# First slots of a two-layer encoder trunk: splits from transposed tiles in PSUM, transposes between products, and squares summed a slot sooner

## The chip, the core and the metric

The kernel runs on one core of one Trainium2 chip. The metric is the device time of one execution in microseconds (us). TensorE (PE) has its weight loads shown apart (PEld); VectorE is DVE, ScalarE ACT, GpSimd POOL, SyncE SP.

## What is computed

Two consecutive layers of a hybrid encoder on 256 tokens, with 16 learned meta tokens ahead of them (T = 272), width 2048, float32. Layer 0 runs 2-D neighbourhood attention and bidirectional mLSTM heads beside each other, layer 1 gated linear attention; each is followed by a gated ConvFFN. Every sub-layer is pre-RMSNorm with a residual add. What matters here are two starts, each a norm followed by a projection:

```python
def _rms(x, gain):
    xf = x.astype(jnp.float32)
    y = xf * lax.rsqrt(jnp.mean(xf * xf, axis=-1, keepdims=True) + EPS)
    return (y * gain.astype(jnp.float32)).astype(x.dtype)

# layer 0:  _split(rms(x) @ w_in, EVEN_SIZES)      the opening: mLSTM columns first
# both layers, _conv_ffn(h, ...):
u = h @ w_up                                       # then a 3-tap convolution over tokens
g, val = jnp.split(acc, 2, axis=-1)
return (jax.nn.silu(g) * val) @ w_down
```

## The kernel before

Activations are kept transposed, features on partitions: `h` is 16 tiles of 128 x 272, the residual. Every float32 operand of a projection is split into a high and a low half: `act_hi` = h x gain rounded (`norm_high`, ACT, L594), `act_lo` = h x gain - act_hi (`norm_low`, DVE, L1046); weights likewise, `w_hi` on ACT (`hi`, L539, writing `hi_done`) and `w_lo` on DVE (`lo`, L942, writing `split_done`). A product is three matmuls, high x high, low x high and high x low (L1455 to L1457). The factor 1/rms per token is left out of the halves; it is applied as each output leaves PSUM (`evac`, L949, by `rstd`), so the sum of squares is needed only then.

A projection runs in iterations of eight slots (`gemm`, `body`). A slot is a weight block of four k tiles by two output tiles, 512 KB in one of four buffers of `raw`: 24 matmuls. For `full` projections slots 0 to 3 make output group 0 (PSUM banks 0 and 1) and slots 4 to 7 group 1 (banks 2 and 3). SP's `fetch` (L405) of a slot waits until the slot four before is split. In slot s of its program ACT makes the high weight half of slot s + 3, DVE the low one. Each engine runs its own queue in order; what runs beside a projection are generators, advanced one step a slot (`side`, `beside`).

In the first iteration behind a norm (`late=True`) the groups leave only in slots 6 and 7, because `rstd` comes late: `norm_side` squares four tiles a slot on ACT (L613), adds them up on DVE one slot after (`sum_squares`, L1063; three long sums, then two short ones), lets PE multiply the sum by ones behind slot 5 (L1498), takes the root on ACT in slot 6 and the reciprocal on DVE in slot 6, ahead of that slot's weight half. `ffn_stage` (L812, L1392, L1765) runs `up00`, `down00` and so on; `NORM_EARLY` says how many tiles of the halves are made in the last iteration of the projection before (8 for norms 1 and 3). A conv exit is long: DVE moves two tiles out of PSUM (L976), ACT applies the middle tap (L558), DVE the two others (L984, L989), and for group 1 ACT's SiLU and DVE's gate and split follow.

The opening: SP loads x in five parts (`X_PARTS`), a weight slot behind each but the first. PE multiplies ones by ones 20 times (`WARM`, L1751), transposes the gains, then turns x tile by tile into PSUM banks 4 to 7 (`turn_in`, L1476; three transposes a tile): tiles 0 to 7 ahead of the products, 8 to 11 behind slot 0 and 12 to 15 behind slot 1. In four rounds DVE copies two tiles into `h` (`fill_h`, L1367) and ACT two (L796); the halves are then made from `h`, and one weight slot is split per round, slots 3 and 4 behind them (L791, L1371). The first iteration's `norm_side(0)` follows, with 11 small DMA issues on ACT's queue (`load_more`, L528), and behind its ones product a matmul group for the gate columns (the tail, L1504).

Of the kernel before, what the change touches and what calls it, by code (L numbers as in the profile page):

```python
# [95 lines left out]
def build(nc, x, meta_tokens, norm_mix, norm_ffn, ab_w_in, ab_gate_bias, ab_q_gain, ab_k_gain,  # L96
# [54 lines left out]
    with ctx:  # L151
# [101 lines left out]
        all_sems = """const_done gain_in warm_ready param_in conv_in tail_in c_tail_in meta_in gup_in hi_done split_done used bank_free u_ready conv_mid gates_done  # L253
# [110 lines left out]
        WARM = 20  # L364
        X_PARTS = [(0, 2), (2, 2), (4, 4), (8, 4), (12, 4)]
# [38 lines left out]
        def _(sp):  # L404
# [17 lines left out]

            for q, (k0, kn) in enumerate(X_PARTS):
                c0, n = k0 * P, kn * P
                sp.dma_start(tok[:, 1:3, c0:c0 + n],
                             bass.AP(x.tensor, x.offset + c0, [[D, P], [P * D, 2], [1, n]])).then_inc(S(f"tok_in{q}"), 16)
                if q:
                    fetch(gemms[0], 0, q - 1, wait=False)
# [75 lines left out]
        def _(act):  # L504
# [60 lines left out]
            def gemm(g, first=None, beside=None, last_beside=None):  # L565
                def body(i, nxt, ni, side=None, late=False):
                    for s in range(8):
# [7 lines left out]
                        if late:  # L575
                            if s >= 6:
                                evac(g, i, s - 6)
                        elif s % g["gs"] == g["gs"] - 1:
                            evac(g, i, s // g["gs"])

                last, start = g["iters"] - 1, 0
                if first:
                    body(0, g, 1, first, late=True)
                    finish(first)
                    start = 1
# [14 lines left out]

            def norm_early(n):
# [11 lines left out]
            def norm_side(n):  # L613

                for q in range(4):
# [3 lines left out]
                    A(sq[:, 4 * q:4 * q + 4, :], h[:, 4 * q:4 * q + 4, :], ACT.Square).then_inc(S("sq_ready"), 1)  # L619
# [5 lines left out]
                yield  # L625
                if n == 2:
# [176 lines left out]
            for s in range(3, 3 + gemms[0]["ahead"]):  # L803
                hi(gemms[0], 0, s)
# [7 lines left out]
            def ffn_stage(layer, n):  # L812
                norm(n)
                gemm(G[f"up{layer}0"], first=norm_side(n))
# [117 lines left out]
        def _(dve):  # L932
# [3 lines left out]
            V.memset(ones[:, :], 1.0).then_inc(S("warm_ready"), 1)  # L936
            dve.sem_inc(S("const_done"), 1)
# [73 lines left out]
            def gemm(g, first=None, beside=None, last_beside=None):  # L1011
                per = 7 if g["evac"] == "conv" else g["ng"] if g.get("wide") else 0

                def body(i, nxt, ni, side=None, late=False):
                    for s in range(8):
# [7 lines left out]
                        if late:  # L1023
                            if s >= 6:
                                evac(g, i, s - 6)
# [4 lines left out]
                if first:  # L1030
                    body(0, g, 1, first, late=True)
# [335 lines left out]
            def fill_h(k):  # L1367
                dve.wait_ge(S("xT_done"), k + 2)
                V.tensor_copy(h[:, k:k + 2, :], ps[:, 4:6, 0:T]).then_inc(S("h_dve"), 1)

            for q in range(4):  # L1371
                fill_h(4 * q)
                if q == 0:
                    dve.wait_ge(S("par_evac"), 1)
# [453 lines left out]
```

## Time and profile before

| | us |
|---|---|
| median of 3 runs | 2412.82 |
| all runs | 2408.90, 2412.82, 2415.22 |
| the profiled execution, device time | 2412.13 |
| its span, first to last instruction | 2410.3 |
| PE busy (products and weight loads overlap) | 2374.9 |
| DVE busy | 1623.4 |
| ACT busy | 1181.4 |
| mean granted TensorE clock, 1 being 2.4 GHz | 0.992 |

Busy shares and the chain are sums over the whole span. To see a start, one reads the timeline of that stretch and engine: each row has the start, the duration, the instruction, and in brackets how long the engine was idle before it and what released it. The table of stretches gives PE's granted clock between two times.

### The profile page before, as it was taken

What the parts mean: (1) busy time and instruction counts of PE and PEld (TensorE: products, weight loads), DVE (VectorE), ACT (ScalarE), POOL (GpSimd) and SP (SyncE); (2) the same over time, 40 slices, a digit from 0 to 9 for tenths busy, and PEclk for the clock granted to TensorE, in tenths of its full rate; (3) what the DMA queues carried; (4) which work ended last, traced back from release to release, by engine and by line L of the source; (5) the groups of instructions that cost most, each with busy time, mean ns of one, the idle gap of its engine ahead of it and who ended that gap; (6) DMA issues with size and microseconds to landing.
All of it is one profiled execution on the core that took longest, in us unless ns stands there. A gap on an engine that the chain in (4) does not pass through costs nothing.

```text
span 2410.3 us, 50498 instructions
## 1 busy us (share of the span) xinstructions
PE 2374.9 (99%) x19342; PEld 2291.6 (95%) x19342; DVE 1623.4 (67%) x2333; ACT 1181.4 (49%) x1563; POOL 34.8 (1%) x78
## 2 busy tenths in 40 slices
PE   9999989999999999999999999999999999999999
PEld 7998887999999999999999999999999999999998
DVE  5447796677765776577574666766777667766774
ACT  5344645554543444454458633454545445544543
POOL 0000001000000000000002000000000000000000
PEclk9999999999999999999999999999999999999999
DMA  6654455555565565655665544456565656666665
GB/s 183 191 145 126 132 144 125 169 167 184 190 201 184 176 207 182 195 182 183 193 182 152 158 123 114 122 155 205 167 200 192 206 185 193 203 200 190 209 194 164
DMA packets 430780, 420.26 MB, mean 174 GB/s; under 512 B 26082, under 2 KB 428812, under 8 KB 430636
## 3 DMA queue, kind: packets, MB, share of 16 engines
q1 hardware_dynamic: 416720, 415.29, 55.9%
q10 hardware_dynamic: 13932, 3.17, 1.2%
q8 instruction: 92, 1.51, 0.3%
q14 instruction: 36, 0.29, 0.0%
HBM read 416.31 MB, written 2.10 MB: 174 GB/s over the span
## 4 chain that ended last, share of the span: by engine, by line
PE 89%; DVE 6%; ACT 3%; issue 2%; ACTq 0%; DVEq 0%
PE ps L1457 27%; PE ps L1455 24%; PE ps L1456 24%; PE ps L1453 6%; DVE w_lo L946 2%; PE ps L1687 1%; ACT w_hi L545 1%; PE ps L1681 1%; PE ps L1526 1%; PE ps L1525 1%; PE ps L1504 1%; DVE rt L1145 1%; DVE rt L1153 1%; PE ps L1527 0%; ACT act_hi L599 0%
## 5 line engine op out<-in xcount | busy, mean ns | idle before, releaser
L1455 PE MATMUL ps<-act_hi,w_hi 128*128 128x272 f32 (+1 forms) x4864 | 1371.3, 282 | 10.2 <-DVE w_lo L946 8.8
L1456 PE MATMUL ps<-act_lo,w_hi 128*128 128x272 f32 (+1 forms) x4864 | 1354.5, 278 | 0.0
L1457 PE MATMUL ps<-act_hi,w_lo 128*128 128x272 f32 (+1 forms) x4864 | 1354.4, 278 | 0.0
L946 DVE TENSOR_TENSOR w_lo<-raw,w_hi 128x1024 fp32r<-128x1024 f32 (+1 forms) x800 | 946.3, 1203 | 477.9 <-ACT w_hi L545 450.0
L545 ACT ACTIVATE w_hi<-raw 128x1024 fp32r<-128x1024 f32 (+1 forms) x797 | 815.4, 1035 | 684.8 <-PE ps L1457 652.1
L1455 PEld LDWEIGHTS ps<-act_hi,w_hi 128*128 128x128 f32 x4864 | 929.0, 191 | 18.6 <-issue 10.0
L1456 PEld LDWEIGHTS ps<-act_lo,w_hi 128*128 128x128 f32 x4864 | 929.0, 191 | 1.5
L1457 PEld LDWEIGHTS ps<-act_hi,w_lo 128*128 128x128 f32 x4864 | 928.8, 191 | 0.0
L1457 PE MATMUL ps<-g_both,w_lo 128*128 128x272 f32 (+1 forms) x1408 | 388.3, 276 | 0.0
L1457 PEld LDWEIGHTS ps<-g_both,w_lo 128*128 128x128 f32 x1408 | 268.2, 190 | 0.0
L1453 PE MATMUL ps<-g_both,w_hi 128*128 128x512 f32 x704 | 231.5, 383 | 0.0
L558 ACT ACTIVATE acc<-un,conv 128x272 f32<-128x272 f32 (+1 forms) x176 | 97.2, 599 | 236.9 <-DVE un L976 236.9
L1455 PE MATMUL ps<-g_both,w_hi 128*128 128x272 f32 x704 | 196.4, 279 | 0.0
L1456 PE MATMUL ps<-g_both,w_hi 128*128 128x272 f32 x704 | 196.4, 279 | 0.0
L984 DVE SCALAR_TENSOR_TENSOR acc<-un,conv,acc 128x271 f32<-128x271 f32 (+1 forms) x176 | 78.9, 490 | 124.5 <-ACT acc L558 124.5
L1453 PEld LDWEIGHTS ps<-g_both,w_hi 128*128 128x128 f32 x704 | 133.1, 189 | 18.2
L1455 PEld LDWEIGHTS ps<-g_both,w_hi 128*128 128x128 f32 x704 | 133.1, 189 | 0.0
L1456 PEld LDWEIGHTS ps<-g_both,w_hi 128*128 128x128 f32 x704 | 133.1, 189 | 0.0
L976 DVE TENSOR_TENSOR un<-ps,rstd 128x544 f32<-128x544 f32 (+1 forms) x88 | 62.4, 709 | 28.2 <-PE ps L1457 27.6
L989 DVE SCALAR_TENSOR_TENSOR acc<-un,conv,acc 128x271 f32<-128x271 f32 (+1 forms) x176 | 78.3, 486 | 0.0
L960 DVE TENSOR_TENSOR h<-ps,h 128x544 f32<-128x544 f32 (+4 forms) x80 | 56.6, 707 | 16.1 <-PE ps L1457 15.2
L1298 DVE TENSOR_TENSOR proj_all<-proj_all,bc 128x272 f32<-128x272 f32 (+1 forms) x112 | 40.8, 421 | 0.0
(250 smaller groups left out, 1182.8 us busy)
## 6 DMA issues: line engine op xcount, KB each, us to landing
raw<-in_ffn_w_up SPq DMA_DIRECT2D x352, 512.0 KB, 4.6
raw<-in_ffn_w_down SPq DMA_DIRECT2D x128, 512.0 KB, 4.2
raw<-in_ab_w_in SPq DMA_DIRECT2D x96, 512.0 KB, 3.8
raw<-in_c_w_in SPq DMA_DIRECT2D x96, 512.0 KB, 3.8
raw<-in_ffn_w_down SPq DMA_DIRECT2D x64, 384.0 KB, 4.0
raw<-in_ab_w_out SPq DMA_DIRECT2D x32, 512.0 KB, 3.4
raw<-in_c_w_out SPq DMA_DIRECT2D x32, 512.0 KB, 4.3
bias<-in_ab_rel_bias ACTq DMA_DIRECT2D x32, 64.0 KB, 5.1
```

The source lines that it names most:

```text
L545: A(w_hi[:, s % 4, 0:kc * 256], raw[:, s % 4, 0:kc * 256], ACT.Copy).then_inc(S("hi_done"), 1)
L558: ins = A(acc[:, grp, m, o0:T], un[:, grp, m, o0:T], ACT.Identity, bias=conv[:, g["layer"], 3, bass.ds(mt, 1)], scale=conv[:, g["layer"], ...
L946: V.tensor_tensor(w_lo[:, s % 4, 0:kc * 256], raw[:, s % 4, 0:kc * 256], w_hi[:, s % 4, 0:kc * 256].bitcast(F32), ALU.subtract).then_inc(S ...
L960: V.tensor_tensor(hh, banks, hh, ALU.add).then_inc(S("bank_free"), 1)
L976: V.tensor_tensor(un[:, grp, :, t0:T], banks, rs, ALU.mult).then_inc(S("u_ready"), 1)
L984: before.append(chain.mark(V.scalar_tensor_tensor(acc[:, grp, m, b1:T], un[:, grp, m, b1 - 1:T - 1], wt[0][:, bass.ds(mt[m], 1)], acc[:, g ...
L989: ins = V.scalar_tensor_tensor(acc[:, grp, m, o0:T - 1], un[:, grp, m, o0 + 1:T], wt[2][:, bass.ds(mt[m], 1)], acc[:, grp, m, o0:T - 1], A ...
L1298: ins = V.tensor_tensor(o, o, total_of(a[d], l, not right), ALU.mult)
L1453: mm(o2, wh, g_both[:, kk, :, :, t0 // 2:].rearrange("p c a b -> p c b a"), start=(c == 0 and k == 0), stop=False)
L1455: mm(o, wh, moving(xh, kk), start=(c == 0 and k == 0), stop=False)
L1456: mm(o, wh, moving(xl, kk), start=False, stop=False)
L1457: ins = mm(o, wl, moving(xh, kk), start=False, stop=end)
```

## The change

In the opening: the 20 products of ones go. x is loaded in eight pairs of tiles, weight slots 0 to 3 behind pairs 0, 2, 4 and 6. PE turns pairs 0 to 2 ahead of the products; pairs 3 to 7 each follow half a slot of products, whose order is changed to two k tiles by two outputs, and half a slot waits for two `act_lo` tiles, not four. Pairs take PSUM banks 4-5, 6-7 and 2-3 in turn. `act_hi` and `act_lo` are made from PSUM; the copies into `h` come behind them (even pairs DVE, odd pairs ACT) and hold the bank. Weight slot 0 is split ahead of the first halves, and each next one a pair or so ahead of its use.

For norms 1 and 3 (`SOON`: `up00` and `up10`): the squares of tiles 0 to 7 and their sum move into slots 4 to 6 of the last iteration of the projection before; squares 2 and 3, the remaining sums, PE's ones product, root and reciprocal come one slot sooner; and group 0 leaves in slot 5 instead of 6 (`SOON_LATE`). Norms 0 and 2 keep their slots.

```diff
-        WARM = 20
-        X_PARTS = [(0, 2), (2, 2), (4, 4), (8, 4), (12, 4)]
+        SOON = (1, 3)
+        LATE, SOON_LATE = {6: 0, 7: 1}, {5: 0, 7: 1}
+        PAIR_BANK = [4 if p % 3 == 0 else 6 if p % 3 == 1 else 2 for p in range(KT // 2)]
+        FETCH_AFTER = {0: 0, 2: 1, 4: 2, 6: 3}
...
@@ SP
-            for q, (k0, kn) in enumerate(X_PARTS):
-                c0, n = k0 * P, kn * P
+            for p in range(KT // 2):
+                c0, n = 2 * p * P, 2 * P
...
-                if q:
-                    fetch(gemms[0], 0, q - 1, wait=False)
+                if p in FETCH_AFTER:
+                    fetch(gemms[0], 0, FETCH_AFTER[p], wait=False)
...
@@ body on ACT and DVE
                         if late:
-                            if s >= 6:
-                                evac(g, i, s - 6)
+                            if s in late:
+                                evac(g, i, late[s])
...
@@ ACT
             def norm_early(n):
...
+                if n in SOON:
+                    for q in range(2):
+                        square(q)
+                        yield
...
             def norm_side(n):
-                for q in range(4):
+                for q in range(2 if n in SOON else 0, 4):
...
                 yield
+                if n in SOON:
+                    yield
...
-            for q in range(4):
-                act.wait_ge(S("h_dve"), q + 1)
-                norm_high(0, 4 * q)
-                norm_high(0, 4 * q + 1)
-                act.wait_ge(S("xT_done"), 4 * q + 4)
-                A(h[:, 4 * q + 2:4 * q + 4, :], ps[:, 6:8, 0:T], ACT.Copy).then_inc(S("h_act"), 1)
-                if q < 3:
-                    act.wait_ge(landed[q], 16)
-                    A(w_hi[:, q, :], raw[:, q, :], ACT.Copy).then_inc(S("hi_done"), 1)
-                act.wait_ge(S("h_act"), q + 1)
-                norm_high(0, 4 * q + 2)
-                norm_high(0, 4 * q + 3)
-            for s in range(3, 3 + gemms[0]["ahead"]):
-                hi(gemms[0], 0, s)
+            def first_high(p):
+
+                act.wait_ge(S("xT_done"), 2 * p + 2)
+                for k in (2 * p, 2 * p + 1):
+                    A(act_hi[:, k, :, :], parted(ps[:, PAIR_BANK[p] + k % 2, 0:T]), ACT.Copy,
+                      scale=vec[:, V_MIX + k:V_MIX + k + 1]).then_inc(S("x_hi"), 1)
...
+            def fill_odd(p):
+
+                act.wait_ge(S("act_ready"), 2 * p + 2)
+                b = PAIR_BANK[p]
+                A(h[:, 2 * p:2 * p + 2, :], ps[:, b:b + 2, 0:T], ACT.Copy).then_inc(S("h_act"), 1)
+
+            first_weights(0)
+            for p in range(KT // 2):
+                first_high(p)
+                if p in (1, 3, 5):
+                    first_weights((p + 1) // 2)
+                if p % 2 == 0 and p:
+                    fill_odd(p - 1)
+            hi(gemms[0], 0, 4)
+            fill_odd(7)
...
@@ DVE
             def norm_early(n):
...
+                if n in SOON:
+                    yield
+                    yield
+                    sum_squares(n, 1)
+                    yield
...
             def norm_side(n):
-                for t in range(6):
-                    if 2 <= t < 5:
-                        sum_squares(n, t - 1)
-                    if t == 4:
+                soon = n in SOON
+                for t in range(5 if soon else 6):
+                    if 2 - soon <= t < 5 - 2 * soon:
+                        sum_squares(n, t - 1 + 2 * soon)
+                    if t == 4 - soon:
                         sum_squares(n, 4)
                         sum_squares(n, 5)
...
+            lo(gemms[0], 0, 0)
+            for p in range(KT // 2):
+                first_low(p)
+                if p in (1, 3, 5):
+                    lo(gemms[0], 0, (p + 1) // 2)
+                if p % 2 == 0:
+                    b = PAIR_BANK[p]
+                    V.tensor_copy(h[:, 2 * p:2 * p + 2, :], ps[:, b:b + 2, 0:T]).then_inc(S("h_dve"), 1)
+            lo(gemms[0], 0, 4)
...
@@ PE
+                        opening = isinstance(n, int) and n == 0 and s < 4
...
+                        pairs = [(m, k) for m in range(2) for k in range(kc)]
+                        if opening:
+                            pairs = [(m, k) for k0_ in (0, 2) for m in range(2) for k in (k0_, k0_ + 1)]
+                        for j, (m, k) in enumerate(pairs):
+                            if opening and j % 4 == 0:
+                                pe.wait_ge(S("act_ready"), k0 + k + 2)
...
+                            if opening and j % 4 == 3 and 2 * s + j // 4 + 3 < KT // 2:
+                                turn_in(2 * s + j // 4 + 3)
...
+            def turn_in(p):
+
+                pe.wait_ge(S(f"tok_in{p}"), 16)
+                if p == 0:
+                    pe.wait_ge(S("meta_in"), 16)
+                if p == 2:
+                    pe.wait_ge(S("par_evac"), 1)
+                if p >= 3:
+                    pe.wait_ge(S("act_ready"), 2 * (p - 3) + 2)
+                    pe.wait_ge(S("h_act" if (p - 3) % 2 else "h_dve"), (p - 3) // 2 + 1)
+                for k in (2 * p, 2 * p + 1):
+                    for tt, (t0, tn) in enumerate(TILES):
+                        ins = tr(ps[:, PAIR_BANK[p] + k % 2, t0:t0 + tn], tok[0:tn, tt, k * P:(k + 1) * P], ident[0:tn, 0:tn])
+                    ins.then_inc(S("xT_done"), 1)
...
             def norm_side(n):
-                for t in range(5):
-                    if n == 0 and t < 2:
-                        for k in range(8 + 4 * t, 12 + 4 * t):
-                            turn_in(k)
+                for t in range(4 if n in SOON else 5):
                     yield
...
-            for n in range(WARM):
-                mm(ps[:, 3, 0:P], ones[:, :], ones[:, :], start=True, stop=True)
...
-            for k in range(8):
-                turn_in(k)
+            for p in range(3):
+                turn_in(p)
```

## Rows read from the trace of the kernel before

**Rows 1.** The page: chain that ended last, shares of the span by engine
```profile
PE 89%; DVE 6%; ACT 3%; issue 2%; ACTq 0%; DVEq 0%
```

**Rows 2.** Waits of TensorE: engine line <- waited for: us in all, times, longest
```profile
PE ps L1455 <- DVE w_lo L946: 8.8, 4, 3.1
```

**Rows 3.** Timeline of PE: start us, us, instruction, idle before and releaser
```profile
30.90 0.35 PE L1455 MATMUL ps<-act_hi,w_hi 128*128 128x272 f32 x1 [2.12 <-DVE w_lo L946]
...
529.14 0.38 PE L1455 MATMUL ps<-act_hi,w_hi 128*128 128x272 f32 x1 [2.68 <-DVE w_lo L946]
...
1344.78 1.35 PE L1681 MATMUL ps<-proj_all 128*16 128x16 f32 x12 [1.67 <-DVE proj_all L971]
...
1725.46 0.58 PE L1455 MATMUL ps<-act_hi,w_hi 128*128 128x258 f32 x1 [3.13 <-DVE w_lo L946]
```

**Rows 4.** Stretches of PE: from:to and us, PE busy (x), granted clock, DMA, GB/s
```profile
7.40:11.20 3.80, 3.50 (x21) 1.00 1.07 388
13.98:18.05 4.07, 4.07 (x18) 0.50 0.79 262
31.70:35.10 3.40, 3.40 (x18) 0.50 0.94 254
...
530.05:533.46 3.41, 3.41 (x17) 0.50 0.82 238
...
1725.46:1731.50 6.04, 6.04 (x28) 0.50 0.72 219
...
1343.00:1352.00 9.00, 7.33 (x66) 1.00 0.44 120
```

**Rows 5.** Timeline of ACT in steady running, after 60 us
```profile
61.12 1.06 ACT L545 ACTIVATE w_hi<-raw 128x1024 fp32r<-128x1024 f32 x1 [1.72 <-PE ps L1457]
```

**Rows 6.** Timeline of DVE in up00, and one row of ACT in up10
```profile
501.07 1.23 DVE L946 TENSOR_TENSOR w_lo<-raw,w_hi 128x1024 fp32r<-128x1024 f32 x1 [1.45 <-ACT w_hi L545]
...
513.92 1.84 DVE L1091 RECIPROCAL rstd<-rstd 128x272 f32<-128x272 f32 x1
...
521.75 0.72 DVE L976 TENSOR_TENSOR un<-ps,rstd 128x544 f32<-128x544 f32 x1
...
1705.16 1.06 ACT L545 ACTIVATE w_hi<-raw 128x1024 fp32r<-128x1024 f32 x1 [1.13 <-DMA raw<-in_ffn_w_up]
```

**Rows 7.** Timeline of PE and ACT in the opening
```profile
1.13 6.26 PE L1752 MATMUL ps<-ones 128*128 128x128 f32 x40 [1.13 <-DVE ones L936]
...
10.26 0.60 ACT L796 ACTIVATE h<-ps 128x544 f32<-128x544 f32 x1
...
11.00 1.63 PE L1485 MATMUL ps<-ident,tok 16*128 16x16 f32 x6 [0.16 <-ACT h L796]
...
13.98 0.57 PE L1455 MATMUL ps<-act_hi,w_hi 128*128 128x272 f32 x1 [1.36 <-DVE act_lo L1050]
...
18.91 2.19 PE L1485 MATMUL ps<-ident,tok 16*128 16x16 f32 x12
```

**Rows 8.** DMA issues in the opening: KB, us from issue (1.30, 1.84) to landing
```profile
tok<-in_meta_tokens ACTq DMA_DIRECT2D x1, 128.0 KB, 5.6
...
raw<-in_ab_w_in SPq DMA_DIRECT2D x1, 512.0 KB, 6.6
```

**Rows 9.** Groups by line and form: xcount | busy us, mean ns
```profile
L599 ACT ACTIVATE act_hi<-h,vec 128x272 fp32r<-128x272 f32 x64 | 31.0, 541 | 12.5 <-DVE h L1369 8.3 <-PE ps L1457 4.2
...
L1050 DVE SCALAR_TENSOR_TENSOR act_lo<-h,vec,act_hi 128x272 fp32r<-128x272 f32 x64 | 28.9, 498 | 3.5 <-ACT act_hi L599 3.5
...
L1129 DVE SCALAR_TENSOR_TENSOR ml_p<-ps,ml_x 128x272 f32<-128x272 f32 x16 | 6.3, 434 | 0.0
```

**Rows 10.** Timeline of DVE and PE at the opening's sums
```profile
32.47 1.29 DVE L1068 TENSOR_TENSOR sq<-sq 128x1088 f32<-128x1088 f32 x1 [0.59 <-ACT sq L619]
...
39.41 1.20 DVE L1071 TENSOR_TENSOR sq<-sq 128x544 f32<-128x544 f32 x2
...
40.98 0.62 PE L1498 MATMUL ps<-sq,ones 128*128 128x272 f32 x2
```

More of the change, by code:

```diff
@@ L582, in gemm @@
                 if first:
-                    body(0, g, 1, first, late=True)
+                    body(0, g, 1, first, late)
                     finish(first)
@@ L599, in norm_high, with square @@
                 A(act_hi[:, k, :, :], parted(h[:, k, :]), ACT.Copy, scale=vec[:, v0 + k:v0 + k + 1]).then_inc(S("x_hi"), 1)
+            def square(q):
+                A(sq[:, 4 * q:4 * q + 4, :], h[:, 4 * q:4 * q + 4, :], ACT.Square).then_inc(S("sq_ready"), 1)
             def norm_early(n):
@@ L618, in norm_side @@
                         act.wait_ge(S("h_act"), q + 1)
-                    A(sq[:, 4 * q:4 * q + 4, :], h[:, 4 * q:4 * q + 4, :], ACT.Square).then_inc(S("sq_ready"), 1)
+                    square(q)
                     if n == 0:
@@ L813, in ffn_stage @@
                 norm(n)
-                gemm(G[f"up{layer}0"], first=norm_side(n))
+                gemm(G[f"up{layer}0"], first=norm_side(n), late=SOON_LATE)
                 gemm(G[f"down{layer}0"])
@@ L1030, in gemm @@
                 if first:
-                    body(0, g, 1, first, late=True)
+                    body(0, g, 1, first, late)
                     finish(first)
@@ L1365, in low_gla, with first_low @@
                                 ALU.subtract).then_inc(S("act_ready"), 1)
[L1367 to L1374, printed above, removed]
[L1375 to L1384 removed]
+            def first_low(p):
+                for k in (2 * p, 2 * p + 1):
+                    dve.wait_ge(S("x_hi"), k + 1)
+                    V.scalar_tensor_tensor(act_lo[:, k, :, :], parted(ps[:, PAIR_BANK[p] + k % 2, 0:T]), vec[:, V_MIX + k:V_MIX + k + 1],
+                                           act_hi[:, k, :, :].bitcast(F32), ALU.mult, ALU.subtract).then_inc(S("act_ready"), 1)
+            lo(gemms[0], 0, 0)
[7 more added lines that the diff above has]
+            lo(gemms[0], 0, 4)
             mixers = even()
@@ L1393, in ffn_stage @@
                 norm(n)
-                gemm(G[f"up{layer}0"], first=norm_side(n))
+                gemm(G[f"up{layer}0"], first=norm_side(n), late=SOON_LATE)
                 gemm(G[f"down{layer}0"])
@@ L1437, in body @@
                             pe.wait_ge(S("bank_free"), i * g["ng"] + (g["gr0"] + grp + 1))
-                        if grp == 0:
+                        opening = isinstance(n, int) and n == 0 and s < 4
+                        if grp == 0 and not opening:
                             if mid:
@@ L1445, in body @@
                             o = ps[:, 2 * (grp % 2) + m, 0:T - t0]
                             o2 = ps[:, 2 * (grp % 2) + m, :].rearrange("p (a b) -> p a b", a=2)
[L1447 to L1457 removed]
+                            kk = g["x0"] + k0 + k
@@ new lines, in body @@
+                            w0 = k * 256 + m * P
+                            wh, wl = w_hi[:, s % 4, w0:w0 + P], w_lo[:, s % 4, w0:w0 + P]
+                            end = c == g["gs"] - 1 and k == kc - 1
+                            if g.get("wide"):
+                                mm(o2, wh, g_both[:, kk, :, :, t0 // 2:].rearrange("p c a b -> p c b a"), start=(c == 0 and k == 0), stop=False)
+                            else:
+                                mm(o, wh, moving(xh, kk), start=(c == 0 and k == 0), stop=False)
+                                mm(o, wh, moving(xl, kk), start=False, stop=False)
@@ L1458, in body @@
+                            ins = mm(o, wl, moving(xh, kk), start=False, stop=end)
+                            if opening and j % 4 == 3 and 2 * s + j // 4 + 3 < KT // 2:
+                                turn_in(2 * s + j // 4 + 3)
                         ins.then_inc(S("used"), 1)
```

55 lines of the change are left out of this document (13 added, 42 removed).

## The prediction

> **What bounds the kernel now.** I began with the chain that ended last on the page [rows 1]: TensorE (PE) holds 89% of it. So a change can win only where PE waits, or where it runs at the lower of its two clock levels. The waits of PE come next [rows 2]: the largest group is its products waiting for VectorE's (DVE's) low half of a weight slot, 8.8 us in four waits, the longest 3.1. Three of these four lie where the change works: 2.12 us at 30.90 in the opening, 2.68 us at 529.14 in `up00`, 3.13 us at 1725.46 in `up10` [rows 3]. Last the clock [rows 4]. It stood at 1.2 GHz (0.50) in the first 4.07 us of products, after an almost product-free stretch with transposes; again from 31.70 to 35.10, from 530.05 to 533.46, and under 6.04 us of products from 1725.46, each time after one of the three waits. A wait of 1.67 us at 1344.78 left it at 2.4 GHz, 1.00 [rows 3, 4]. One product takes about 0.116 us at the high level and 0.227 at the low one (18 products in 4.07 us [rows 4]); a slot of 24 takes 2.78, in steady running one weight half of 1.06 on ScalarE (ACT) and 1.72 idle before it [rows 5].
>
> **Two up projections (`SOON`).** In `up00` the waiting chain is on DVE: three sums of squares (1.28 each) and two short ones (1.20 together, durations from [rows 10]) lie in slots 2 to 4, the reciprocal in slot 6, then both output groups leave in slots 6 and 7. The second group's exit starts at 521.75 [rows 6]; behind it, ACT's and DVE's conv steps and the SiLU comes the weight half of the next iteration's slot 3, on which PE waited until 529.14 [rows 3]. The change moves one sum and two squares ahead of the projection, into slots where ACT sits idle 1.72 us of each 2.78 [rows 5] and DVE similarly; a square is 1.09, so it is hidden. If that cover were gone it would cost 1.1. The moved sum (1.28) stands before one weight half that is wanted two slots later: nothing. In the projection the sums then end one slot sooner, PE's ones product and the square root follow one slot sooner, and the reciprocal starts as soon as DVE is through. Laid out again with the same durations: from 502.3, the end of the weight half that starts at 501.07 [rows 6], two sums, four weight halves of 1.2 and the two short sums, 8.6 us, so the reciprocal starts at 510.9 instead of 513.92; it ends at 512.7 and a weight half at 513.9; the first group's exit with its conv steps lasts 3.6 (exit 0.72, ACT's steps 1.1 with hand-overs, DVE's 1.75) to 517.5; two weight halves to 520.0; second exit from 520.0 instead of 521.75. That is 1.75 us sooner; PE's wait becomes 2.68 - 1.75 = 0.9. The second exit cannot start before PE ends slot 7, at about 529.14 - 2.68 - 3 x 2.78 = 518.1; that bound does not decide. The same lay-out for `up10`, with 0.1 us less per slot and one weight transfer wanted just when it lands, gives 1.65 us and leaves 1.5.
>
> Both remaining waits are shorter than the 1.67 us that left the clock alone, so I let the two falls go: 3.41 us at half speed cost 1.7, 6.04 us cost 3.0. Sum: 1.75 + 1.65 + 1.7 + 3.0 = 8.1 us gained. Its ends: 3.4 if the clock falls all the same, 8.1 if not; a little above if other runs fell for longer.
>
> **The opening.** Removed: the 20 warm-up products (6.26 us of PE until 7.39), PE otherwise having nothing to do. They did not carry to the products: the clock was still full from 7.4 to 11.2, over transposes, and half at 13.98 [rows 4, 7]. What next sets the start? The meta tokens land at 1.30 + 5.6 = 6.9 [rows 8], so the transposes start near 7.0 in place of 7.41, and at the low clock: a pair of tiles takes 1.45 (the last pair starts at 11.00 and its last end is 1.63 later) against 1.0 at the high one (four tiles in 2.19 with the last drain, from 18.91) [rows 7]. SP now issues the first weight slot as its second transfer, 0.5 us sooner and behind 256 KB instead of 512; it landed at 1.84 + 6.6 = 8.4 before [rows 8], I take 7.5 (ends 7.2 and 8.4). Then on ACT high weight half 1.05 to 8.55, act_hi pair 0.97 to 9.5; on DVE the low weight half 8.57 to 9.8 and act_lo pair 0.91 to 10.7. The first product needs two act_lo tiles and not four: 10.75 instead of 13.98 (11.65 at the late end). Reading the tiles out of PSUM instead of `h` changes two operands; no row shows act_hi or act_lo made so. Nearest rows: DVE's two-operand step from PSUM at this width 0.43 against 0.50 for act_lo from `h` [rows 9]; ACT's copy from PSUM at double width 0.60 against 0.54 for act_hi from `h` [rows 7, 9]. So -0.1 to +0.1 each, taken as nothing (the DVE row is the nearest). The copies into `h` leave the path to act_hi but still stand in the queues (0.60 on ACT [rows 7]; on DVE 0.72, as the exit of that width [rows 6]).
>
> From 10.75 PE runs half a slot (12 products, 1.39 or 2.72 by the clock), a pair of transposes, and so on five times, until pair 7 is turned. DVE needs about 1.9 us a pair (act_lo 0.91, half a copy 0.36, half a weight split 0.6), less than PE's 2.4, so PE sets this stretch. SP's fetches of slots 4 to 7 wait for splits that come sooner or as soon as they are wanted. I take two rounds at the low clock and three at the high: 10.75 + 2 x 4.17 + 3 x 2.39 = 26.25.
>
> Now the step that eats the gain. Behind the last transposes ACT still has act_hi (0.97), the high half of slot 4 (1.05), the last copy (0.60) and two squares (2.0): 26.4 + 4.6 = 31.0. From the first sum to the end of the last DVE took 32.47 to 40.61, with waits for ACT that stay [rows 10]: 8.1. So PE's ones product, at 40.98 now, comes at about 39.3. PE itself would be there 1.39 + 3 x 2.78 after 26.25, at 36.0: about 3.3 us sooner, in two waits, one before slot 5 and one of about 2 before the ones product. Of the 3.2 us won at the start, the 2.12 us wait and the low clock from 31.7, only 40.98 - 39.3 = 1.7 us are seen. Behind a wait of about 2 us the clock can fall, over the tail product and slots 6 and 7: 1.7 to 3.0 by the rows, at about an even chance; I charge 1.0. The opening: 0.7 us gained.
>
> **The sum.** 2412.13 (the profiled execution; span 2410.3 and 1.8 around it, 0.7 below the median of the runs) - 8.1 - 0.7 = 2403.3; by the median 2404.0. Forecast 2403.5, its own range 2400 to 2406.5.
>
> **Rivals.** (a) The low clock lasts through the whole interleaved stretch. For: before, the level rose only under products in one piece (4.07 us, 3.40 us, 6.04 us [rows 4]); now they come in pieces of 2.7 us with transposes between, and over the transposes from 7.4 it fell. Against: the transposes between full-speed slots at 18.91 [rows 7] did not make it fall. Then pair 7 is turned at 10.75 + 5 x 4.17 = 31.6, the ones product comes at 31.75 + 4.6 + 8.25 = 44.6, 3.6 us later than before, and 2412.1 - 8.1 + 3.6 = 2407.6.
>
> The Trainium skill, page TensorE: Matmul & The Clock Gate, Part 4: PE-mode transpose, says that transposes do not count as busy time for the clock in the way products do. By that rule the clock stays low as in this rival; the trace agrees in that the level fell during them, but it does not show whether they help to raise it. The same page's table under Why this matters for your kernels advises warming up with products first, which speaks against dropping them; here the level had fallen before the first product, so the trace does not agree for this kernel.
>
> (b) The clock falls in the up projections even after the shorter waits; for it, one of them is 1.5 against 1.67 known to be harmless. Only the 3.4 of shorter waiting are won: 2412.1 - 3.4 - 0.7 = 2408.0.
>
> (c) The change does not do what it says there: the second group's exit, or the weight half behind it, is set by PE or by a transfer and not by the sums, and the waits stay. For: in `up10` ACT waited 1.13 us for a transfer at 1705.16. Against: DVE's row of the second exit in `up00` shows no idle time before it, so it waited for neither [rows 6]. 2412.1 - 0.7 = 2411.4.
>
> (d) Slower than before: the pieces keep the clock at the low level not only to pair 7 but, with the waits before slot 5 and the ones product breaking the run again, to the end of the first iteration. Eight slots at 5.44 (43.5), five turns (7.3), the tail product doubled (14.9) and about 1.6 besides end at 78 instead of 55.3: 22.8 us later, 2426.8. It decides once the clock has not risen by the stretch from the last turn through slot 4, over 9 us of products; every such stretch in the rows raised it, so the chance is small.
>
> **Chances.** Forecast 0.45, (a) 0.31, (b) 0.12, (c) 0.08, (d) 0.04. The range 2399.5 to 2410.5 takes in the forecast, (a) and (b) with the bounds of the unknowns (0.9 for the first landing, 2 for a fall of the clock) and leaves out (c), (d) and the edges. A measurement tells about 0.3%, 7.2 us, from no change: faster means under 2405.6. From the forecast 0.38, from (a) 0.08, from (b) 0.02: faster 0.48; slower 0.05 with (d); within 0.3%: 0.47.
>
> **What would show it.** In the opening: first product near 10.8, then in the clock of the stretch 11 to 32 which level the interleaved stretch had; the ones product near 39.3 (forecast) or 44.6 (a), and PE waiting for the low half of slot 5 and for the sums. In `up00` and `up10`: second exit 1.7 us sooner against the projection's first product, waits of 0.9 and 1.5, and clock 1.00 behind them. I am wrong in mechanism if the ones product follows the first product's gain in full, if the sums are not what holds PE there, or if the two short waits end in a fall.

## The result, and the profile after

The changed kernel took 2400.14 us (median of 5 runs, 2398.64 to 2404.30) against 2412.92 for the kernel before (5 runs, 2408.90 to 2415.22): a ratio of 0.995, 95% interval 0.9936 to 0.9965. Run once more beside others it took 2402.93 (6 runs) against 2412.37, a ratio of 0.9964 (0.9952 to 0.9976). The forecast was 2403.5 with a range of 2399.5 to 2410.5. The profiled execution of the changed kernel is the slowest of its five, 2404.3 with a span of 2402.6, so the two profiles lie only 7.7 us apart.

The page's busy shares and chain of the changed kernel (in its code the three matmuls of a product are L1488 to L1490, the weight halves L970 and L547, and `turn_in` is L1523):

```profile
PE 2366.1 (98%) x19302; PEld 2282.2 (95%) x19302; DVE 1622.6 (68%) x2333; ACT 1180.7 (49%) x1563; POOL 34.6 (1%) x78
...
PE 90%; DVE 6%; ACT 2%; issue 1%; ACTq 1%; DMA 0%; DVEq 0%
```

These shares hardly differ from those before: 90% for 89% of PE in the chain, 98% for 99% busy. What differs is PE's waits. They are in the next view, to be set beside [rows 2]:

```profile
PE ps L1488 <- DVE w_lo L970: 4.1, 4, 1.4
PE ps L1787 <- DMA stage<-in_norm_mix: 4.0, 1, 4.0
PE ps L1523 <- DMA tok<-in_meta_tokens: 3.2, 1, 3.2
...
PE ps L1533 <- DVE sq L1100: 1.9, 1, 1.9
```

The waits for the low weight half went from 8.8 us to 4.1; 3.8 of these 4.7 us lie in the two up projections, the rest in the opening. New are two waits for transfers at the start, where the products of ones stood, and 1.9 us before the ones product. The timeline of PE in the opening (start, duration, instruction, idle time before it), beside [rows 3, 7, 10]:

```profile
7.47 5.04 PE L1523 MATMUL ps<-ident,tok 16*128 16x16 f32 x18 [3.19 <-DMA tok<-in_meta_tokens]
12.16 0.57 PE L1488 MATMUL ps<-act_hi,w_hi 128*128 128x272 f32 x1
12.53 0.43 PE L1489 MATMUL ps<-act_lo,w_hi 128*128 128x272 f32 x1
12.76 0.43 PE L1490 MATMUL ps<-act_hi,w_lo 128*128 128x272 f32 x1
...
15.16 1.49 PE L1523 MATMUL ps<-ident,tok 16*128 16x16 f32 x6
16.41 0.36 PE L1488 MATMUL ps<-act_hi,w_hi 128*128 128x272 f32 x1
...
25.32 1.13 PE L1523 MATMUL ps<-ident,tok 16*128 16x16 f32 x6
26.20 0.36 PE L1488 MATMUL ps<-act_hi,w_hi 128*128 128x272 f32 x1
...
34.63 0.38 PE L1488 MATMUL ps<-act_hi,w_hi 128*128 128x272 f32 x1 [1.24 <-DVE w_lo L970]
39.63 0.79 PE L1533 MATMUL ps<-sq,ones 128*128 128x272 f32 x2 [1.95 <-DVE sq L1100]
...
55.66 0.36 PE L1488 MATMUL ps<-act_hi,w_hi 128*128 128x272 f32 x1
```

The first products start 1.8 us sooner than in [rows 7] and at the low level: 12.53 and 12.76 are 0.23 apart. From the second half slot on, the rounds of 12 products and 6 transposes are 2.45 apart (16.41, 18.86 and so on), the high level. Then PE waits twice, and the last row, the first product of iteration 1, is 0.39 us *later* than in the kernel before (55.27 there). In this execution the whole opening gave nothing. The stretches of PE's clock say why, and what became of the up projections; beside [rows 4]:

```profile
40.10:43.50 3.40, 3.40 (x16) 0.50 0.36 97
527.90:533.00 5.10, 4.51 (x39) 1.00 0.57 173
1719.20:1725.00 5.80, 4.36 (x39) 1.00 0.50 153
```

Behind the two waits of the opening the clock was at 1.2 GHz for 3.4 us. Behind the waits of `up00` and `up10` it stayed at 2.4 GHz. The rows of `up00` on DVE and PE, and PE's wait in `up10`, beside [rows 3, 6]:

```profile
512.13 1.85 DVE L1121 RECIPROCAL rstd<-rstd 128x272 f32<-128x272 f32 x1
...
515.15 0.72 DVE L1000 TENSOR_TENSOR un<-ps,rstd 128x544 f32<-128x544 f32 x1
...
521.10 0.72 DVE L1000 TENSOR_TENSOR un<-ps,rstd 128x544 f32<-128x544 f32 x1
...
528.50 0.38 PE L1488 MATMUL ps<-act_hi,w_hi 128*128 128x272 f32 x1 [0.59 <-DVE w_lo L970]
...
1720.67 0.38 PE L1488 MATMUL ps<-act_hi,w_hi 128*128 128x258 f32 x1 [1.44 <-DVE w_lo L970]
```

Read from the last residual exit ahead of each projection (495.42 and 1691.64 before, 496.91 and 1689.33 after), the 7.7 us of span between the profiles split up as follows. To 496.91 the changed kernel is 1.5 us behind: 0.4 from the opening and 1.1 from stages that the change doesn't touch, where it spent 17.1 us at the low level and the kernel before 13.7. From `up00` to `up10` it wins 3.8: 2.1 of wait and 1.7 of clock. From `up10` to the end it wins 5.4: 1.7 of wait, 3.0 of clock, 0.7 left over.

Where do the falls in the untouched stages come from? Here is one of them in the kernel before, PE's row and the stretch behind it, and the same fall in the changed kernel:

```profile
164.54 0.19 PE L1546 MATMUL ps<-ident,row_m 4*16 4x4 f32 x2 [2.30 <-ACT row_f L680]
164.80:171.60 6.80, 6.80 (x35) 0.50 0.51 145
```

```profile
166.40:173.20 6.80, 6.80 (x32) 0.50 0.61 163
```

This wait of 2.30 us stands in all 12 profiles of this study, at 159 to 165 us, and in all 12 the clock falls 0.3 to 2.6 us after its end, for 3.4 or 6.8 us. Another wait, of 2.4 to 2.8 us on DVE's `proj_all` (it ends at 356.52 in the kernel before), has a fall beginning inside it or up to 1.6 us behind it in nine of the 12. So waits of PE of more than 2 us elsewhere in the kernel come with falls too, and behind some of them a fall comes in one run and not in another.

### The profile page after: what moved, and what is told of

It reads as the page before. It is cut to its first block, busy times and chain, and to the rows that moved or that the text cites. A ratio compares the mean times of both kernels' runs of the same rounds, so it can differ in the third digit from the quotient of the medians.

```text
span 2402.6 us, 50407 instructions
## 1 busy us (share of the span) xinstructions
PE 2366.1 (98%) x19302; PEld 2282.2 (95%) x19302; DVE 1622.6 (68%) x2333; ACT 1180.7 (49%) x1563; POOL 34.6 (1%) x78
## 4 chain that ended last, share of the span: by engine, by line
PE 90%; DVE 6%; ACT 2%; issue 1%; ACTq 1%; DMA 0%; DVEq 0%
PE ps L1490 27%; PE ps L1488 24%; PE ps L1489 24%; PE ps L1486 6%; DVE w_lo L970 2%; PE ps L1722 1%; ACT w_hi L547 1%; PE ps L1561 1%; PE ps L1560 1%; PE ps L1716 1%; PE ps L1539 1%; DVE rt L1175 1%; PE ps L1562 1%; DVE rt L1183 1%; PE ps L1523 0%
## 5 line engine op out<-in xcount | busy, mean ns | idle before, releaser
L1488 PE MATMUL ps<-act_hi,w_hi 128*128 128x272 f32 (+1 forms) x4864 | 1369.5, 282 | 4.1 <-DVE w_lo L970 4.1
L1490 PE MATMUL ps<-act_hi,w_lo 128*128 128x272 f32 (+1 forms) x4864 | 1352.4, 278 | 0.0
L970 DVE TENSOR_TENSOR w_lo<-raw,w_hi 128x1024 fp32r<-128x1024 f32 (+1 forms) x800 | 945.9, 1203 | 480.0 <-ACT w_hi L547 446.9
L547 ACT ACTIVATE w_hi<-raw 128x1024 fp32r<-128x1024 f32 (+1 forms) x796 | 813.6, 1035 | 681.0 <-PE ps L1490 647.3
L1488 PEld LDWEIGHTS ps<-act_hi,w_hi 128*128 128x128 f32 x4864 | 927.0, 191 | 11.8 <-issue 5.5
L1490 PEld LDWEIGHTS ps<-act_hi,w_lo 128*128 128x128 f32 x4864 | 926.9, 191 | 0.0
L1490 PE MATMUL ps<-g_both,w_lo 128*128 128x272 f32 (+1 forms) x1408 | 388.3, 276 | 0.0
L1490 PEld LDWEIGHTS ps<-g_both,w_lo 128*128 128x128 f32 x1408 | 268.2, 190 | 0.0
L1488 PE MATMUL ps<-g_both,w_hi 128*128 128x272 f32 x704 | 196.4, 279 | 0.0
L1488 PEld LDWEIGHTS ps<-g_both,w_hi 128*128 128x128 f32 x704 | 133.1, 189 | 0.0
```

Of the source, the lines that this page charges most:

```text
L547: A(w_hi[:, s % 4, 0:kc * 256], raw[:, s % 4, 0:kc * 256], ACT.Copy).then_inc(S("hi_done"), 1)
L970: V.tensor_tensor(w_lo[:, s % 4, 0:kc * 256], raw[:, s % 4, 0:kc * 256], w_hi[:, s % 4, 0:kc * 256].bitcast(F32), ALU.subtract).then_inc(S ...
L1488: mm(o, wh, moving(xh, kk), start=(c == 0 and k == 0), stop=False)
L1490: ins = mm(o, wl, moving(xh, kk), start=False, stop=end)
```

## Experiments

Each run was timed beside the kernel before, on the same chip, in three sessions: again, soon_only, opening_only and ahead in the first, longer, meta_first, warm_back and ahead2 in the second, ahead2_b and ahead2_warm in the third. The medians of the kernel before were 2412.37, 2411.95 and 2412.64. Ratios are to these, with 95% intervals. The changed kernel itself stood only in the first; a comparison of it with runs of the other two is across sessions.

### The changed kernel once more (again), and each half of it alone (soon_only, opening_only)

`soon_only` is the kernel before with the edits for `SOON` alone. `opening_only` is the changed kernel with

```diff
-        SOON = (1, 3)
-        LATE, SOON_LATE = {6: 0, 7: 1}, {5: 0, 7: 1}
+        SOON = ()
+        LATE, SOON_LATE = {6: 0, 7: 1}, {6: 0, 7: 1}
```

> The changed kernel once more, as a second profile of it and as the partner of the three runs beside it. The medians of the two kernels lie 12.8 us apart, their profiles only 7.7 us of span. Theory A (the sum of the prediction: 8.1 us in the two up projections, next to nothing in the opening; the rest is where the clock happens to fall elsewhere): this profile again shows waits of about 0.6 and 1.4 us in up00 and up10 with the clock at 1.00 behind them, the ones product of the opening near 39.8, and the median is 10 to 13 us below before. Theory B (the opening gives about 5 us and the first profile was an odd one): the first iteration of the opening ends some 5 us before 55.3.

> Only the squares and sums of the two up projections moved; the opening is that of before. Theory A: 8 us faster than before (range 6.5 to 10), that is 60% or more of the whole change. Theory B (the opening carries half of the gain): 5 to 7 us faster.

> Only the opening changed; squares and sums of the two up projections stay where they were. Theory A: between 1 us slower and 3 us faster than before, with waits of about 2.7 and 3.1 us in up00 and up10 and the clock at 0.50 behind at least one of them. Theory B: 5 us faster.

Measured: again 2402.93 (0.9964, 0.9952 to 0.9976), soon_only 2403.25 (0.9971, 0.9960 to 0.9983), opening_only 2410.46 (0.9992, 0.9983 to 1.0001). So the up projections give 9.1 us of the medians and the opening 1.9 alone, which its interval can't tell from nothing, or 0.3 on top of the other. soon_only and opening_only came out inside what theory A said of them. For the changed kernel itself theory A was only half right: the waits of the second profile are 0.63 and 1.55 with the clock at 1.00 behind them, but its median is 9.4 us below the kernel before and not 10 to 13, and its ones product comes at 37.55 and not near 39.8. Theory B falls with soon_only: half of the gain was never in the opening.

PE in the second profile of the changed kernel, where the meta tokens land sooner:

```profile
5.47 1.71 PE L1523 MATMUL ps<-ident,tok 16*128 16x16 f32 x6 [1.54 <-DMA tok<-in_meta_tokens]
7.43 3.40 PE L1523 MATMUL ps<-ident,tok 16*128 16x16 f32 x12 [0.25 <-DMA tok<-in_x]
10.48 0.57 PE L1488 MATMUL ps<-act_hi,w_hi 128*128 128x272 f32 x1
...
37.55 0.70 PE L1533 MATMUL ps<-sq,ones 128*128 128x272 f32 x2 [1.95 <-DVE sq L1100]
...
51.92 0.36 PE L1488 MATMUL ps<-act_hi,w_hi 128*128 128x272 f32 x1
```

The same program starts its transposes at 5.47 and not at 7.47, its ones product comes 2.1 us sooner behind the same two waits (1.15 and 1.95), here no fall of the clock follows, and iteration 1 starts at 51.92. From the ones product to there it is 14.4 us against 16.0 in the first profile: 1.7 us is what the fall costs. Of six profiles with the changed kernel's waits in the opening (the changed kernel twice, opening_only, warm_back, longer, meta_first) two show the fall, 0.4 later and 0.8 us sooner than 55.27; the four others start iteration 1 between 51.87 and 52.13, 3.1 to 3.4 us sooner. (These are differences to one profile of the kernel before; in soon_only, which has the same opening as that kernel, iteration 1 starts at 54.87, 0.4 sooner.)

PE in opening_only, the waits in `up00` and `up10` and the stretches behind them:

```profile
527.60 0.59 PE L1488 MATMUL ps<-act_hi,w_hi 128*128 128x272 f32 x1 [2.69 <-DVE w_lo L970]
...
1723.44 0.38 PE L1488 MATMUL ps<-act_hi,w_hi 128*128 128x258 f32 x1 [2.78 <-DVE w_lo L970]
```

```profile
527.40:530.80 3.40, 3.21 (x14) 0.50 0.54 161
...
1723.50:1728.00 4.50, 4.50 (x40) 1.00 0.65 198
```

With the sums where they were, the long waits are back. One is followed by the low level, the other, 0.1 us longer, is not. In soon_only the waits are 0.63 and 1.44, with the clock at 1.00 behind both.

### A longer wait on purpose (longer)

```diff
                         sum_squares(n, 4)
                         sum_squares(n, 5)
+                        if soon:
+                            V.tensor_tensor(sq[:, 8:12, :], sq[:, 4:8, :], sq[:, 4:8, :], ALU.add)
+                            V.tensor_tensor(sq[:, 12:16, :], sq[:, 4:8, :], sq[:, 4:8, :], ALU.add)
```

> The changed kernel with two more additions of 1.28 us on VectorE behind the short sums of up00 and up10, written to tiles that nobody reads any more: the suspected wait made longer, and nothing else. If the sums on VectorE hold PE and a wait beyond some 2 us costs the clock too: waits of 3.1 and 4.0 us instead of 0.6 and 1.4, 0.50 behind both, and 8 to 11 us slower than the changed kernel. If only the waits count and the clock falls for reasons of its own: 5 us slower. If VectorE's queue there does not set the time: no difference.

Measured: 2408.98 (10 runs; 0.9985, 0.9974 to 0.9997), 9 us above the changed kernel's first median and 6 above its second. PE in its profile, waits and the stretches behind:

```profile
526.97 0.38 PE L1491 MATMUL ps<-act_hi,w_hi 128*128 128x272 f32 x1 [2.56 <-DVE w_lo L970]
...
1721.54 0.38 PE L1491 MATMUL ps<-act_hi,w_hi 128*128 128x258 f32 x1 [2.59 <-DVE w_lo L970]
```

```profile
527.00:532.00 5.00, 5.00 (x43) 1.00 0.69 211
...
1721.60:1727.00 5.40, 5.40 (x49) 1.00 0.72 209
```

The expected waits of 3.1 and 4.0 us did not come in full, and neither did a fall of the clock. But DVE's queue there does set PE's time: with two smaller waits that appeared earlier in the same projections (0.15 and 0.60), the waits add up to 2.7 and 3.2 instead of 0.6 and 1.4, 3.9 us more. That is less than the 5.1 put in, so about 1.2 of the additions was covered. The time lies between what was expected for waits alone (5 us) and for waits and falls (8 to 11). The ten runs lie in two groups, four from 2402.6 to 2405.8 with a mean clock of 0.996 to 0.999 and six from 2408.8 to 2410.8 with 0.994 to 0.995: this would fit falls behind the longer waits in six of ten runs, but only one run left a trace, and it is one of the four, so that is not shown. What the trace shows is that a wait of 2.6 us need not end in a fall.

### Squares and sums ahead in the opening too (ahead, ahead2, ahead2_b)

`ahead`, the core of the edit:

```diff
@@ ACT, opening @@
+                if p in (2, 4):
+                    act.wait_ge(S("h_dve"), p // 2)
+                    act.wait_ge(S("h_act"), p // 2)
+                    square(p // 2 - 1)
@@ ACT, norm_side @@
-                        load_more(q)
+                        load_more(q - 2)
                     yield
                 if n == 0:
+                    load_more(2)
+                    yield
+                    load_more(3)
+                    yield
                     load_more(4)
@@ DVE, opening @@
             lo(gemms[0], 0, 4)
+            sum_squares(0, 1)
@@ DVE, norm_side @@
+                    if n == 0:
+                        if t in (1, 3):
+                            sum_squares(0, 2 if t == 1 else 3)
+                        if t == 3:
+                            sum_squares(0, 4)
+                            sum_squares(0, 5)
```

`ahead2` also splits slot 5 in the opening:

```diff
-    add("ml_in", ab_w_in[0], full, 6, "store", col0=24 * P, p0=24, ready=0, ahead=2)
+    add("ml_in", ab_w_in[0], full, 6, "store", col0=24 * P, p0=24, ready=0, ahead=3)
@@ ACT, opening @@
             fill_odd(7)
+            hi(gemms[0], 0, 5)
@@ DVE, opening @@
             sum_squares(0, 1)
+            lo(gemms[0], 0, 5)
```

> The changed kernel, and in the opening too squares of tiles 0 to 7 are made by ScalarE in its idle time before pairs 3 and 5, their sum follows the low half of slot 4 on VectorE, and the last sums stand before the low half of slot 6. Theory A says that the chain of squares and sums takes back what the early start wins (1.2 us of wait before slot 5 and 1.9 us before the ones product, then 3.4 us at half clock): the ones product comes at 36.2 to 37.2 instead of 39.8, both waits are under 1 us, the clock stays at 1.00 behind them, and the median is 3 to 5 us below the changed kernel. Rival: PE or the weight transfers of slots 5 to 7 set that time anyway: within 1 us of the changed kernel.

> As the run named ahead, and slot 5 of the weights is split in the opening too, behind the last copy into h. There ScalarE's high half of slot 5 waited 1.4 us for its own queue of DMA issues and PE 1.2 us for the low half. Expected if that queue is the cause: no wait of PE before slot 5, the ones product 1 us sooner against the first transpose than in ahead (30.0 us behind it there), clock at 1.00 from the first rise to the end of the first iteration, median 1 us below ahead or the same; if the transfer of slot 5 or 6 is the cause, the wait stays.

> The kernel of the run named ahead2 once more, as partner of the next. Expected: 2396 to 2398.5 us again, 14 to 16 us below before; in the profile no wait of PE over 0.6 us between the first product and the end of iteration 0.

Measured: ahead 2400.33 (2399.38 to 2401.54; 0.9954, 0.9941 to 0.9967), 2.6 us below the changed kernel beside it (3 to 5 were expected). ahead2 2396.91 (2395.87 to 2398.68; 0.9940, 0.9927 to 0.9954) and, once more, 2398.35 (0.9941, 0.9928 to 0.9953). ACT and PE in ahead:

```profile
30.41 0.38 ACTq L528 DMA_DIRECT2D stage<-in_ffn_conv_b  x1
30.82 0.78 ACTq L528 DMA_DIRECT2D stage<-in_ffn_conv_w  x2
31.70 1.06 ACT L547 ACTIVATE w_hi<-raw 128x1024 fp32r<-128x1024 f32 x1 [1.36 <-issue]
...
34.14 0.38 PE L1503 MATMUL ps<-act_hi,w_hi 128*128 128x272 f32 x1 [1.21 <-DVE w_lo L978]
37.02 0.62 PE L1548 MATMUL ps<-sq,ones 128*128 128x272 f32 x2
```

and PE in ahead2:

```profile
34.70 0.62 PE L1550 MATMUL ps<-sq,ones 128*128 128x272 f32 x2
35.78 0.38 PE L1505 MATMUL ps<-act_hi,w_hi 128*128 128x272 f32 x1 [0.45 <-DVE w_lo L979]
...
49.72 0.36 PE L1505 MATMUL ps<-act_hi,w_hi 128*128 128x272 f32 x1
```

In ahead the wait before the ones product is gone (37.02 instead of 39.63, with the first transpose 0.5 us sooner), but the one before slot 5 is as long as ever. ACT's row suggests its cause: 1.36 us in which it waited for nothing but its own queue, where six of the eight small transfers of conv rows still stood to be issued (the last three at 30.41 and 30.82) without squares beside them. ahead2 confirms it: with slot 5 split ahead of them that wait is gone, the ones product stands 28.0 us behind the first transpose instead of 30.0 (29.0 was expected), and iteration 1 starts at 49.72, 2.2 to 5.9 us sooner than in any profile of the changed opening. In ahead2_b it starts at 49.60, and PE's longest wait from the first product to there is 0.46. This is the fastest kernel of the study, with or without the products of ones of the next section: 14 to 15 us below the kernel before it. The changed one is 9.4 to 12.8 below, so this is worth some 1.5 to 5.6 us across sessions; the expectation was 1 us or less below ahead, and by the ratios it is 3.

### The products of ones put back (warm_back, ahead2_warm)

```diff
             pe.wait_ge(S("const_done"), 3)
+            for n in range(20):
+                mm(ps[:, 3, 0:P], ones[:, :], ones[:, :], start=True, stop=True)
             pe.wait_ge(S("gain_in"), 16)
```

> The changed kernel with the 20 products of ones put back ahead of the transposes (PE busy with them from about 1.1 to 7.4 us). Theory A: they keep the clock at the high level while pairs 0 to 2 are turned, so a pair takes 1.0 us and not 1.7, but they also hold the transposes until 7.4 even where the meta tokens land at 5.5; the first product comes at 10.6 to 11.2 every time, the clock then falls under it and rises again among the interleaved transposes, and the median is within 1.5 us of the changed kernel. Theory B (warming up first pays): 2 us or more faster than the changed kernel. Theory C (they cost their own time): 3 us or more slower.

> The kernel of ahead2 with the 20 products of ones put back. In warm_back they gave a high clock to the transposes of pairs 0 to 2 (3.2 us for three pairs against 5.0) and to the first products, but the gain was lost in the waits before slot 5 and before the ones product, which ahead2 has shortened. If so the first product comes at 12 us with the clock at 1.00 and, PE being the bound from there on, iteration 0 ends 1 to 2.7 us sooner (one half slot at the high level instead of the low one is 1.3): median 2394.5 to 2396.5. Rival: ScalarE and VectorE, or the landings of x and the weights, cap the interleaved stretch: the same as ahead2 within 0.7 us, or slower, since the products of ones hold PE until 8.4.

Measured: warm_back 2399.45 (2396.53 to 2402.92; 0.9952, 0.9936 to 0.9967), ahead2_warm 2398.12 (0.9939, 0.9927 to 0.9951) against 2398.35 for ahead2 beside it. PE in warm_back:

```profile
8.46 3.22 PE L1523 MATMUL ps<-ident,tok 16*128 16x16 f32 x18
12.17 0.35 PE L1488 MATMUL ps<-act_hi,w_hi 128*128 128x272 f32 x1 [0.49 <-DVE act_lo L1401]
```

Three pairs take 3.22 us at the high level instead of 5.04, but they start at 8.46, a microsecond later than their data in the slowest landing. Then DVE's act_lo becomes the limit, and the products start at 12.17, not at 10.6 to 11.2 as expected. Part of this is the place: the products of ones stand here behind the wait for the identity, start at 1.59 and end near 8.4; in the kernel before they stood ahead of that wait, started at 1.13 and were through by 7.39. The projection's products start at the high level, as a duration of 0.35 for the first one tells (0.57 without), which wins back what the late start loses. The fall that I expected under them didn't come. On the changed kernel the median is 0.7 us under its first and 3.5 under its second measurement, inside their scatter of 6 to 7 us. On ahead2, where nothing behind hides a gain, it is 0.2, the rival's verdict, and iteration 1 started at 49.41 with them and at 49.60 without. In this place the products of ones neither cost nor bring anything. In their old place, a microsecond earlier, no run tried them with the new opening; there they may bring something.

### The meta tokens first (meta_first)

```diff
+            act.dma_start(tok[0:META, 0, :], meta_tokens[:, :]).then_inc(S("meta_in"), 16)
             for v, n in rows_of:
...
-                if at == 0:
-                    act.dma_start(tok[0:META, 0, :], meta_tokens[:, :]).then_inc(S("meta_in"), 16)
```

> The changed kernel with one move: ScalarE issues the transfer of the meta tokens as its first and not as its second. In four profiles their landing, at 5.3 to 7.3 us, was what PE's first transpose waited for. Theory A (this landing sets when the opening starts, and its scatter is part of the scatter of the runs): landing 0.5 us sooner at least, iteration 1 starts sooner by as much, median 0.5 to 2 us below the changed kernel. Rival (the chain behind it, weights and squares, sets the time): no difference.

Measured: 2402.93 (2397.25 to 2404.28; 0.9960, 0.9945 to 0.9975), no different from the changed kernel (0.9964). PE there:

```profile
5.93 0.28 PE L1786 MATMUL ps<-ident,stage 32*128 32x32 f32 x1 [5.93 <-DMA stage<-in_norm_mix]
6.04 5.04 PE L1522 MATMUL ps<-ident,tok 16*128 16x16 f32 x18
```

The transfer of the gains now came second, and it landed at 5.9 in place of 3.6 to 4.2: PE waits for the one instead of the other, and iteration 1 starts at 51.87, beside 51.92 to 52.13 in the other profiles without a fall. The landing of the first transfers does set when the opening starts, but which of the two is issued first moved it by nothing that the runs can tell.

## Why the prediction was right, step by step

**What bounds PE there: right.** The waits for low weight halves in `up00` and `up10` shrank by 3.8 us, and soon_only, opening_only and longer show DVE's queue in `up00` and `up10` to be the cause, in both directions.

**The second exit 1.75 and 1.65 us sooner: right, a little small.** From the last residual exit to it the trace has 26.33 before and 24.19 after in `up00`, 26.26 and 24.12 in `up10`: 2.14 in both. My reciprocal would have started at 512.4 on the new time scale (510.9 plus the 1.5 by which the stage began later); it started at 512.13. PE's waits are 0.59 and 1.44 for a forecast of 0.9 and 1.5. The squares and the sum that moved cost nothing, as said: the moved sum ran at 491.99, and PE waited for nothing in the 30 us up to the wait of 0.59.

**Two falls of the clock gone, 4.7 us: right for this pair of profiles, and near in size for the medians, though not as a rule.** No fall followed the waits of 0.6 and 1.4 to 1.6 in any of the nine profiles that have waits of that size in place of the long ones. But a long wait doesn't always bring a fall: the two of the kernel before did (2.68 and 3.13), and of the four of 2.6 to 2.8 in opening_only and longer only one. That both fell in the profile I forecast from was in part luck. What the medians won is 9.1 us with 3.8 of waits in it; the fastest runs of soon_only and of the kernel before beside it are only 3.9 us apart (2402.27, 2406.12). The waits are the sure part. The other 5 us would be falls that used to come in most runs and now don't; the one profile of each kernel can't show how often, so this part is argued and not shown. Nothing speaks for my rival (b), a fall behind the shorter waits.

**The start of the opening: the step that failed.** I took the first product at 10.75, from the chain of ACT and DVE, and left PE's own queue out of it: pairs 1 and 2 stand ahead of the products. Three pairs took 5.04 us, 1.68 each and not 1.45, so even by my own 7.0 and 1.45 it would have been 11.35. The meta tokens landed anywhere from 5.3 to 7.3 us, and the first product came at 10.46 to 12.16 in the eight profiles without products of ones. Four of them have it between 10.46 and 10.75, but only because their transposes could start at 5.5 to 6.0 and not at 7.0: where the forecast of 10.75 is hit, it is by luck. That act_hi and act_lo cost nothing more out of PSUM was right: pairs of 0.87 and 0.90 for 0.97 and 0.91.

**The interleaved stretch: right in sum, but by luck, two errors that cancel.** I had two rounds at the low level and the last transposes done at 26.25; they were done at 26.2, with one round at the low level behind a later start. Rival (a), the low level throughout, didn't occur: in each of the profiles with interleaving the products ran at the high level from the first or second round on. In the Trainium skill, page TensorE: Matmul & The Clock Gate, Part 4: PE-mode transpose, stands that transposes do not count as busy time for the clock as products do. These traces do not contradict it, but its consequence as I drew it, that transposes between products would keep the clock low, did not come: in the first profile the level rose at 16.2, while a pair of them was being turned.

**The chain of squares and sums: right.** The ones product at 39.63 for a forecast of 39.3, the first sum at 30.84 for 31.0, two waits of 1.24 and 1.95 for "one before slot 5 and one of about 2". From the end of the last transposes to the ones product I had 13.05 us; it is 13.4 in the first profile and 13.3 in the second. ahead and ahead2 show that this chain held PE: with it shortened, the ones product comes 30.0 and 28.0 us behind the first transpose and not 32.1. But one of my own signs of a wrong mechanism was that the ones product follows the first product's gain in full, and by its letter it came true: in the second profile the first product comes 3.50 us sooner than in the kernel before and the ones product 3.43. The sign was badly chosen. The chain hangs on the last pair turned, which moves with the start, so a start won does pass through. What the chain takes is the rest: in place of the 2.12 us of wait and the fall of the clock in the old opening stand the waits of 1.24 and 1.95.

**The fall behind these waits: right as a chance.** I charged 1.0 for an even chance at 1.7 to 3.0. It came in two of six profiles and cost 1.7. So the opening is worth 3.1 to 3.4 us without it and -0.4 to 0.8 with it, where I had said 0.7; opening_only measured 1.9, with an interval that takes in zero.

**The sum.** Forecast 8.8 us below the profile of before; measured 9.4 and 12.8 by the medians of two sessions. What is left is scatter: within one kernel, runs differ by 2 to 11 us, and in most of them the runs with the lower mean clock are the slower ones (kernel before: 2405.9 and 2406.7 at 0.996, 2416.5 at 0.990). In the profiles most further falls lie between 160 and 380 us, where the change doesn't reach, several of them behind PE's waits of 2.3 to 3.1 us there. How often each comes is known from 12 profiles and no more.

## What to carry to other kernels

Waits taken out at the head of a stage are worth only what the next chain lets through: lay out the queue behind them (here act_hi, weight half, copy, squares, sums) before counting the gain, and move that chain's pieces into idle time first. When an engine's own queue holds independent work ahead of the wanted instruction, take the later of the two chains, its own and the others'. A wait of TensorE of 2.1 to 3.1 us, as here, can be worth more than its length, since the clock fell behind most of them, for 3.4 or 6.8 us and at a price of 1.7 or 3.0. One profile doesn't tell whether a given wait costs that; take more than one, and the medians of the runs.

## What the runs showed of the hardware

Transposes run faster at the high clock level: three pairs of tiles in 3.22 us against 5.04. Landing times of the first transfers scatter from run to run of the same program: 128 KB issued at 1.3 us took 4.0 us in one profile and 6.0 in another. The granted clock in the table of stretches reads 1.00 before the first change in the trace even where the products are 0.23 us apart, as from 12.2 in the changed kernel; the spacing of the products is what tells the level there. One and the same wait of 2.30 us near 160 us was followed by a fall in 12 profiles of 12, but two waits of nearly equal length, 2.69 and 2.78 us in one execution, were followed by a fall and by none.
